# Output projection in column halves with the samples' tile first, and half of the fourth expert slot loaded in between

## What is computed

```
def finish_layer(x, o_nsa, o_dn, g1, sh2, sc2, g2, lp):
    x = x + g1 * (jnp.concatenate([o_nsa, o_dn], axis=-1) @ lp['w_out'])
    return x + g2 * hier_moe(modulate(x, lp['norm_ffn_g'], sh2, sc2), lp)

def modulate(x, g, shift, scale):
    return rmsnorm(x, g) * (1 + scale) + shift

def hier_moe(h, lp):
    lg = x @ lp['router_group_w'] + lp['router_group_b']      # 4 groups, the best one is taken
    le = x @ lp['router_expert_w'] + lp['router_expert_b']    # 8 experts in it, the best two are taken
    ...
    for e in range(32):
        he = silu(x @ lp['w_gate'][e]) * (x @ lp['w_up'][e])
        y = y + gates[:, e:e + 1] * (he @ lp['w_down'][e])
```

## Time and profile before

| what | value |
|---|---|
| median of 3 runs | 1028.65 us (1025.32 to 1033.83) |
| the profiled execution's own time | 1032.61 us |
| its span in the trace | 1030.7 us |
| PE busy | 953.2 us, 92% |
| DVE, ACT, POOL busy | 438.6, 315.3, 281.8 us |
| moved by DMA | 212 MB |
| mean granted clock of the tensor engine | 0.973 of 2.4 GHz |

### The profile page before, as it was taken

How to read it: one execution, slowest core, us unless ns; L and a number is a source line. 1 busy time by engine, 2 the same in 40 slices (tenths; PEclk the granted TensorE clock), 3 DMA queues, 4 the chain that set the end, 5 groups by cost and what they waited for, 6 DMA issues and landing times. The chain is left out here.

```text
span 1030.7 us, 21027 instructions
## 1 busy us (share of the span) xinstructions
PE 953.2 (92%) x8032; PEld 615.2 (60%) x8032; DVE 438.6 (43%) x937; ACT 315.3 (31%) x713; POOL 281.8 (27%) x403
## 2 busy tenths in 40 slices
PE   6899999999799999899899999999899999999795
PEld 5456777777566766787455665455455555555441
DVE  2131000002658345577678762446522333333237
ACT  5100000000646423244577542111022232333244
POOL 7000000033100337920456432000223343434213
PEclk9899999999999999999999999999899998899898
DMA  9975742713650038000744254928699999999972
GB/s 311 353 270 201 261 163 82 163 53 113 221 187 7 1 42 178 20 4 8 190 121 125 70 198 160 302 97 320 225 363 381 386 396 375 385 376 376 370 281 102
DMA packets 90506, 212.16 MB, mean 206 GB/s; under 512 B 31730, under 2 KB 54954, under 8 KB 76510
## 3 DMA queue, kind: packets, MB, share of 16 engines
q1 hardware_dynamic: 77666, 187.36, 53.3%
q0 software_dynamic: 9984, 20.15, 6.0%
q10 hardware_dynamic: 2756, 3.27, 0.9%
HBM read 254.83 MB, written 33.95 MB: 280 GB/s over the span
## 5 line engine op out<-in xcount | busy, mean ns | idle before, releaser
L592 PE MATMUL PS<-hT,wring 128*128 128x288 f32 x256 | 83.6, 408 | 0.0
L2492 POOL DMA_INDIRECT ys_dram<-late,ids x47 | 43.4, 924 | 146.2 <-ACT late L2728 120.1
L593 PE MATMUL PS<-hT,wring 128*128 128x288 f32 x256 | 83.0, 406 | 0.0
L2927 DVE COPY mixT<-PS 128x128 f32<-128x128 f32 x49 | 14.3, 292 | 159.9 <-PE PS L2607 159.9
L2486 POOL DMA_INDIRECT mixT<-h_dram,ids x49 | 47.3, 966 | 105.6 <-DVE ids L2894 87.6
L2588 PE MATMUL PS<-ring,mixT 128*64 128x256 f32 x304 | 71.9, 391 | 2.2 <-DVE mixT L2913 2.2
L2589 PE MATMUL PS<-ring,mixT 128*64 128x256 f32 x304 | 71.9, 391 | 0.0
L2588 PEld LDWEIGHTS PS<-ring,mixT 128*64 128x64 f32 x304 | 42.7, 142 | 31.9 <-issue 10.9
L592 PEld LDWEIGHTS PS<-hT,wring 128*128 128x128 f32 x256 | 48.2, 190 | 17.2 <-DVE xc L203 2.6
L593 PEld LDWEIGHTS PS<-hT,wring 128*128 128x128 f32 x256 | 48.6, 190 | 13.4
L2520 PE MATMUL PS<-late,mixT 128*128 128x512 f32 x128 | 55.5, 593 | 0.9 <-PEq L3013 0.9
(11 more groups left out here) (591 smaller groups left out, 2172.7 us busy)
## 6 DMA issues: line engine op xcount, KB each, us to landing
ring<-in_expert_w_gate_dram SPq DMA_DIRECT2D x27, 1024.0 KB
ring<-in_expert_w_up_dram SPq DMA_DIRECT2D x27, 1024.0 KB
ring<-in_expert_w_down_dram SPq DMA_DIRECT2D x27, 1024.0 KB
late<-in_w_ada_dram SPq DMA_DIRECT2D x8, 2048.0 KB
mod_r<-in_expert_w_gate_dram SPq DMA_DIRECT2D x9, 1024.0 KB
mod_r<-in_expert_w_up_dram SPq DMA_DIRECT2D x9, 1024.0 KB
mod_r<-in_expert_w_down_dram SPq DMA_DIRECT2D x9, 1024.0 KB
late<-in_expert_w_gate_dram SPq DMA_DIRECT2D x7, 1024.0 KB
```

What stands on the lines that cost most here:

```text
L592: MM(PS[:, b, 0:HALF], lhs, hT[:, k, 0:HALF], **s)
L593: last = MM(PS[:, b + 1, 0:HALF], lhs, hT[:, k, HALF:NTOK], **s)
L2492: pool.indirect_dma_start(m.ys_dram.ap(), bass.IndirectOffsetOnAxis(ap=ids[:, 1, j:j + 1], axis=0), yr(n), None, bounds_check=LAST_ROW, oo ...
```

## The change

`w_out` is kept in `late` as two halves of 512 columns, one behind the other, instead of eight full rows of 1024. The projection is done in nine steps (`STEPS`): the whole sample tile, then the first column half of tiles 0 to 3, then the second half of tiles 0 to 3. Each step takes one PSUM bank, in turn, and `y_ps` and `x2_ok` count steps. The later work on a tile (`LINE`) takes the sample tile first, then tiles 0 to 3; a prompt tile can be modulated only after its second half. SP loads gate and up of slot 3 when five steps are done (the first column half of `w_out` is then free) and down after all nine. The issue order of all transfers is as before.

```diff
 def w_out_parts(m):
-    return m.late[:, :].rearrange("p (c n) -> p c n", c=8)
+    return m.late[:, :].rearrange("p (h c n) -> p h c n", h=2, c=8)
...
+        LINE = [PT] + list(range(PT))
+        STEPS = [(PT, 0)] + [(i, half) for half in range(2) for i in range(PT)]
+        whole = lambda i: 1 if i == PT else TILES + 1 + i
...
             sp.wait_ge(y_ps, TILES)
-            load_base(3)
+            load_gate_up(3)
+            sp.wait_ge(y_ps, len(STEPS))
+            load_down(3)
...
-            def y(i):
-                r, b = ROWS[i], 2 * (i % 2)
-                if i >= 2:
-                    pe.wait_ge(x2_ok, i - 1)
+            def y(s):
+                i, half = STEPS[s]
+                if s >= 4:
+                    pe.wait_ge(x2_ok, s - 3)
...
-            for i in range(TILES):
-                y(i)
-                if i >= 2:
-                    logits(i - 2)
-                if i:
-                    turn_rows(i - 1)
+            for s in range(len(STEPS)):
+                y(s)
+                if s == 2:
+                    turn_rows(0)
+                elif s == 3:
+                    logits(0)
+                elif s >= TILES + 1:
+                    if s >= TILES + 2:
+                        logits(s - TILES - 1)
+                    turn_rows(s - TILES)
...
+            def residual(s):
+                i, half = STEPS[s]
+                r, v = ROWS[i], VAR[i]
+                cols = slice(half * HALF, (half + 1) * HALF) if i < PT else slice(0, D)
+                if half == 0:
+                    dve.wait_ge(x_in[i], 16)
+                dve.wait_ge(y_ps, s + 1)
                 if i < PT:
...
                 else:
+                    dve.wait_ge(mods_in, 16 * NB)
                     dve.wait_ge(rw_ok, 1)
...
-            for i in range(TILES):
-                dve.wait_ge(x_in[i], 16)
-                if i == PT:
-                    dve.wait_ge(mods_in, 16 * NB)
-                residual(i)
-                if i:
-                    turned(i - 1)
-                modulated(i)
-                if i >= 2:
-                    take_logits(i - 2)
+            for s in range(len(STEPS)):
+                residual(s)
+                if s == 1:
+                    modulated(0)
+                elif s == 2:
+                    turned(0)
+                elif s == 3:
+                    take_logits(0)
+                elif s >= TILES:
+                    j = s - TILES + 1
+                    if j >= 2:
+                        turned(j - 1)
+                    modulated(j)
+                    if j >= 3:
+                        take_logits(j - 2)
```

More of the change, by code:

```diff
@@ L2274, in load_w_out @@
         cols = slice(half * 512, (half + 1) * 512)
-        sp.dma_start(w_out_parts(m)[:, :, cols], t["w_out"][0].rearrange("(c p) n -> p c n", p=P)[:, :, cols]).then_inc(m.wo_in[half], 16)
+        sp.dma_start(w_out_parts(m)[:, half], t["w_out"][0].rearrange("(c p) n -> p c n", p=P)[:, :, cols]).then_inc(m.wo_in[half], 16)
 def stage_moe(nc, m, sb, sem, t, outs):
@@ L2509, in _ @@
             MM = nc.tensor.matmul
-            def y(i):
-                r, b = ROWS[i], 2 * (i % 2)
-                if i >= 2:
-                    pe.wait_ge(x2_ok, i - 1)
+            def y(s):
+                i, half = STEPS[s]
+                if s >= 4:
+                    pe.wait_ge(x2_ok, s - 3)
                 if i < PT:
+                    for c in range(8):
+                        last = MM(PS[:, s % 4, :], m.mixT[:, c, i * P:(i + 1) * P], wo[:, half, c, :], start=(c == 0), stop=(c == 7))
+                else:
                     for half in range(2):
[L2517 to L2521, removed]
+                        pe.wait_ge(m.wo_in[half], 16)
                     for c in range(8):
                         for half, side in enumerate((R, Q)):
-                            last = MM(PS[side, b, :], m.mixT[:, c, i * P:i * P + r], wo[:, c, half * HALF:(half + 1) * HALF], start=(c == 0), stop=(c == 7))
+                            last = MM(PS[side, s % 4, :], m.mixT[:, c, i * P:i * P + ROWS[i]], wo[:, half, c, :], start=(c == 0), stop=(c == 7))
                 last.then_inc(y_ps, 1)
             def turn_rows(j):
-                r = ROWS[j]
+                i = LINE[j]
+                r = ROWS[i]
                 pe.wait_ge(h_ok, j + 1)
@@ L2532, in turn_rows @@
                 for k in range(KD):
-                    last = nc.tensor.transpose(PS[:, 4 + k // 4, (k % 4) * P:(k % 4) * P + r], h2[0:r, j, k * P:(k + 1) * P], m.ident[0:r, 0:r])
+                    last = nc.tensor.transpose(PS[:, 4 + k // 4, (k % 4) * P:(k % 4) * P + r], h2[0:r, i, k * P:(k + 1) * P], m.ident[0:r, 0:r])
                 last.then_inc(hT_ps, 1)
             def logits(j):
-                r = ROWS[j]
+                r = ROWS[LINE[j]]
                 pe.wait_ge(hT_ok, j + 1)
@@ L2703, in _ @@
             act.dma_start(rb[:, NG:], t["router_expert_b"][0].partition_broadcast(P)).then_inc(rw_in, 16)
-            for i in range(TILES):
+            for j, i in enumerate(LINE):
                 r = ROWS[i]
                 if i == PT:
-                    act.wait_ge(y_ps, TILES)
+                    act.wait_ge(y_ps, 1)
                     act.wait_ge(rw_ok, 1)
-                    nc.scalar.copy(h2[R, PT, HALF:D], PS[Q, 2 * (PT % 2), :]).then_inc(split_ok, 1)
-                act.wait_ge(x2_ok, i + 1)
+                    nc.scalar.copy(h2[R, PT, HALF:D], PS[Q, 0, :]).then_inc(split_ok, 1)
+                act.wait_ge(x2_ok, whole(i))
                 nc.scalar.activation(h2[0:r, i, :], m.x2[0:r, i, :], ACT.Square, accum_out=ssq[0:r, 0, i:i + 1]).then_inc(sq_ok, 1)
-                act.wait_ge(sq_ok, i + 1)
+                act.wait_ge(sq_ok, j + 1)
                 nc.scalar.activation(ssq[0:r, 1, i:i + 1], ssq[0:r, 0, i:i + 1], ACT.Sqrt, scale=1.0 / D, bias=m.eps[0:r, 0:1]).then_inc(rt_ok, 1)
-            for i in range(TILES):
+            for j, i in enumerate(LINE):
                 r = ROWS[i]
-                act.wait_ge(h_ok, i + 1)
+                act.wait_ge(h_ok, j + 1)
                 act.dma_start(m.h2_dram.ap()[i * P:i * P + r, :], h2[0:r, i, :]).then_inc(h_out, 16)
@@ L2798, in modulated, with take_logits @@
                 V.tensor_tensor(h2[0:r, i, :].rearrange("r (k p) -> r p k", k=KD), by_p(ht[0:r, :]), by_p(mod[0:r, v, 1, :]), ALU.add).then_inc(h_ok, 1)
-            def take_logits(i):
+            def take_logits(j):
+                i = LINE[j]
                 r = ROWS[i]
-                dve.wait_ge(lg_ps, i + 1)
-                V.tensor_tensor(lg[0:r, i, :], PS[0:r, 6 + i % 2, 0:NG + NE], rb[0:r, :], ALU.add).then_inc(lg_ok, 1)
+                dve.wait_ge(lg_ps, j + 1)
+                V.tensor_tensor(lg[0:r, i, :], PS[0:r, 6 + j % 2, 0:NG + NE], rb[0:r, :], ALU.add).then_inc(lg_ok, 1)
             dve.wait_ge(pch, 24)
```

23 lines of the change are left out of this document (10 added, 13 removed).

## The result

The changed kernel takes 1044.91 us (median of 4 runs, 1043.18 to 1046.63) against 1031.24 us of the kernel before, timed beside it (median of 4 runs, 1025.32 to 1035.01). The ratio is 1.0137, with a 95% interval of 1.0089 to 1.0184: slower by about 1.4%, with no change well outside the interval. The profiled execution took 1043.68 us, with a span of 1042.0 us.

What follows compares the result with a forecast made beforehand. The tensor engine was taken to bound the projection, with the experts' weight stream close to it later; 12.2 (wait) + 0.1 (work around) + 2.5 (clock) + 0 (slot 3) = +14.8 us on 1028.65 gave 1043.4 us, range 1034 to 1050.

Steps and rivals of the forecast that it cites:

- the sum: Whole kernel: wait, work around it, clock and slot 3 together add 14.8 us, giving 1043.4 us from the median.
- The landing of the sample sequences' rows: Start of the projection stage: the samples' modulation rows, 768 KB in eight transfers, land at 655 us.
- Rival 1: Start of the stage: modulation rows land at 647 to 650, wait only 4 to 7 us, 1035 to 1038; chance 0.12.
- The wait: Before the first transpose: the tensor engine idles 12.2 us until the sample tile is modulated.
- No further wait for prompt tiles: Later projection steps: a prompt tile's 6.4 us chain ends inside the 6.87 us step, otherwise up to 1 us.
- Rival 3: Behind the first wait: low clock over several steps or delayed transposes cost 4 to 8 us more, 1047 to 1052; chance 0.12.
- The clock: Tensor engine behind the first wait: runs at its lower clock for a while, losing 2.5 us, bounds 1 to 4.
- The products: Projection: same number of passes, but less transpose and logits work ahead of the last y, saving 0.75 us.
- The last tile: End of the stage: a full prompt tile now comes last instead of the samples, about +0.9 us.
- The early load of slot 3: Weight stream: fetching 2 MB of slot 3 earlier gains 0, since DMA is nearly idle before the first refill.
- Rival 2: Weight stream: the early 2 MB shorten it by 5.5 us, time about 1028, faster or not slower; chance 0.08.
- The median: Base of the forecast: the kernel before at 1028.65 us, to which 14.8 us were added.

Runs made afterwards that it cites:

- `mid`: Changed kernel with the sample tile's products as the fourth of nine steps instead of the first; 1028.32 us, ratio 0.9979.
- `whole_first`: Kernel before with only its order of tiles changed, sample tile first, prompt tiles whole, slot 3 loaded after all tiles; 1043.51 us, ratio 1.0152.
- `ring_after`: Changed kernel with SP waiting for the samples' modulation rows before loading the first three experts; 1052.89 us, ratio 1.0143.
- `slot3_late`: Changed kernel with gate and up of slot 3 loaded only after all nine steps; 1048.95 us, ratio 1.0190.
- `fill`: Changed kernel with 12 products that nobody reads ahead of the tensor engine's first transpose; 1044.48 us, ratio 1.0127.
- `fill2`: Changed kernel with 17 products that nobody reads ahead of the tensor engine's first transpose; 1055.06 us, ratio 1.0178.
- `spread`: Changed kernel with the samples' modulation rows in eight transfers, each to partitions 8 apart from eight different source rows; 1049.6 us, ratio 1.0128.
- `mods_first`: Changed kernel with the samples' x and modulation rows issued ahead of the prompt's modulation rows and x; 1040.45 us, ratio 1.0118.
- `mid_again`: `mid` unchanged, run once more beside its twin that loads slot 3 late; 1028.28 us, ratio 0.9972 to the kernel before.
- `before_again`: Kernel before, unchanged, traced a second time; 1027.42 us for this one execution.

## Why the prediction was right

1043.4 us (1034 to 1050) was predicted, with 0.78 on slower; 1044.91 us and a ratio of 1.0137 were measured. To the kernel before it is 13.7 us where the sum had 14.8. The mechanism is shown, by its absence in `mid` and by its presence in `whole_first`. By steps:

- **The landing of the sample sequences' rows.** Predicted at 655, 24.0 us after the start of the stage; measured 23.3 us behind the tensor engine's start. The dent in the DMA rate was read rightly, though not all of it is moving: in `ring_after` next to nothing is moved in the last 2.5 us. Rival 1, rows at 647 to 650, fell: in `ring_after` the transfers are as late with nothing beside them. Five traces with the same transfers in the same order (the changed kernel, `whole_first`, `slot3_late`, `fill`, `fill2`) give 23.5 to 26.5 us from SP's start, so the place is good to a few microseconds only.
- **The wait.** 12.2 us predicted, 11.05 measured. Of the 1.15 us between them 0.7 are the earlier landing; 0.2 are the tensor engine's later arrival (650.68, 21.0 us after its start, against 20.8); and the 0.2 booked for signals were in the prices already, since the chain from the rows to the transpose took 8.8 us with them (652.93 to 661.73; 2.5 + 2.8 + 3.5 predicted).
- **No further wait for prompt tiles.** Right, at the margin of 0.4 us: none shows behind the first, nor in `mid`. Rival 3 fell with it.
- **The clock.** 2.5 us predicted, with 1 to 4 as bounds; 3.2 measured (9.97 and 1.11 us for the step and the transpose, against 7.13 and 0.71 in these places in `fill2`). I took the loss behind a wait of 4.73 us for one behind 11 us. The length of the wait doesn't order the losses: the step behind it took 9.28 us behind a wait of 12.8 us (`slot3_late`), 9.95 behind 11.6 (`ring_after`), 8.74 behind 10.0 (`spread`), 9.35 behind 7.9 (`mods_first`) and 8.74 behind 3.8 (`fill`). That is 1.6 to 2.8 us over 7.13, and the term was as good as one execution allows.
- **The products.** 0.75 us saved was predicted, 0.4 is what shows: in `mid_again`, where nothing waits, the last y ends 67.9 us after the tensor engine's start of the stage, against 68.3 before. The halves that run one by one take 7.03 to 7.13 us each, and a whole tile took 13.90. In the changed kernel the last y ends 82.2 us after the start (711.82 less 629.66), against 68.3 before (699.33 less 631.02), which is +13.85, and 11.05 + 3.2 - 0.4 is the same.
- **The last tile.** +0.9 predicted. From the last y to the last logits it is +1.5, with 0.2 of low clock in it (2.20 us for the logits, 1.98 in `mid_again`). But from there to the refill it is 2.4 us less than in the first trace of before, and 1.4 less than in `before_again`. The one microsecond between the two is the low clock in the choice of experts of the first trace (the row of 8.25 us above, 5.42 in the second). The 1.4 fit the wait of 1.59 us for gathered rows, which `before_again` has and the changed kernel doesn't: what the changed kernel pays for its last tile, the kernel before pays for this wait. That is read from the traces, no run tests it. Against `before_again` the refill is 14.1 us later, against the first trace 13.15; the sum was 14.8. The prediction had neither the low clock of its own base trace nor this wait in it, and between them they are the largest part of the difference.
- **The early load of slot 3.** 0 predicted. DMA has little to do ahead of the first refill, and the loop keeps its length, as I said. In the runs it lies between -0.4 and +0.5%, with both signs seen; whether it is exactly nothing stays open. Rival 2 fell: the kernel is slower by 13.7 us.
- **The median.** 14.8 us on a base of 1028.65. The sum was 1.1 us above the measured difference of 13.7 us, and the base 2.6 us below the median measured beside the changed kernel; the errors partly cancel, and that 1043.4 lies only 1.5 us from 1044.91 is in part luck.

What beats both kernels is `mid`: 0.9972 [0.9955, 0.9989] of the kernel before in 12 runs, some 0.3%. Its tensor engine never waits in the projection and has the 0.4 us of the moved products; where the rest of the 2.6 us between the medians comes from, the traces don't settle.

## What to carry to other kernels

Before work is moved to the front of a stage, ask when its data lands, and look for it even where no row shows it: an operand that was read last has been late for free. A dip in the DMA rate with all engines busy marked transfers that are slow by themselves; reordering the queue handed their lateness to what was then behind them, while giving their consumer three more steps of other work cost nothing.

## What was not expected of the hardware

- Eight transfers of 96 KB, each to 8 partitions, move at 94 to 97 GB/s alone in the queue, at a DMA share of 0.51 to 0.53, that is 11 to 12 GB/s for a busy engine, against 24 in the experts' loop. Why each is slow isn't settled: the pattern of partitions and the common source row are excluded as the main cause by `spread`.
- After the last bytes of these transfers more than 2 us went by until the instructions that wait for them began (`ring_after`: a share of 0.03 from 653 on, SP at 655.42, DVE at 655.63).
- They slow what is queued behind them: the prompt's modulation rows landed after 16.7 us instead of 6.9.
- The landing of the same transfers in the same order varied between executions from 23.5 to 26.5 us after the start of the stage, and the time of the experts' loop by 3 us (285.0 and 288.0 for the same kernel).
- Timings of one kernel differ between sets: the kernel before took 1030.79, 1039.24 and 1030.89 us in the three sets. The record gives one chip number for the second and the third, so that the chip makes the difference isn't shown. The experts' loop is where most of it goes: from the first refill to the end 285 to 288 us in the first and third set, 293.0 to 296.6 in the second.
